# Expert weights in a four-slot ring in the order of use, and two narrow projections in column tiles

## The reference, cut to what matters

```python
h = rmsnorm(x, attn_norm)
parts = split(h @ w_in)              # 7448 columns: attention, GLA, DeltaNet, gates
merged = sum over three branches of sigmoid(gate_b) * (y_b @ w_br_b)
x = x + merged @ w_o
h = rmsnorm(x, ffn_norm)             # router: one of 4 groups, then 2 of its 8 experts
x = x + sum over the two experts e of weight * (silu(h @ w_gate_e[e]) * (h @ w_up_e[e])) @ w_down_e[e]
x = x + sigmoid(rmsnorm(x, ple_norm) @ w_ple_gate) * (p_i @ w_ple)
```

## Time and profile before

| | us |
|---|---|
| median of 3 runs | 1855.69 |
| lowest and highest | 1835.51, 2714.79 |
| profiled execution | 1843.19 |
| its span | 1841.5 |

### The profile page before, as it was taken

One profiled execution on the slowest core, in us unless ns is written; L12 is line 12 of the kernel. 1 busy time (PEld: TensorE's weight loads), 2 busy tenths in 40 slices (PEclk: granted clock), 3 DMA queues, 4 the chain that ended last, 5 costly groups with the idle time before them and its releaser, 6 DMA issues.

```text
span 1841.5 us, 19673 instructions
## 1 busy us (share of the span) xinstructions
PE 1456.5 (79%) x7340; PEld 720.6 (39%) x7341; DVE 395.5 (21%) x756; ACT 218.4 (12%) x417; POOL 38.0 (2%) x36
## 2 busy tenths in 40 slices
PE   7999999997655665566889999999976656665678
PEld 6657645452211221122476676454422212221223
DVE  3342514143000000000233425141420000000002
ACT  2121312110000000000211223111100000000001
POOL 0012000000000000000000110000000000000000
PEclk9999999998888888888989999999988888888889
DMA  7332033389999999999442320333899999999992
GB/s 249 114 137 92 1 137 137 115 353 365 402 410 409 410 410 410 409 410 407 156 145 92 137 92 6 142 127 137 349 364 410 410 409 410 410 410 409 410 398 87
DMA packets 153499, 501.19 MB, mean 272 GB/s; under 512 B 13763, under 2 KB 16229, under 8 KB 152293
## 3 DMA queue, kind: packets, MB, share of 16 engines
q1 hardware_dynamic: 153140, 498.72, 69.7%
q0 software_dynamic: 304, 1.76, 0.2%
HBM read 499.37 MB, written 1.05 MB: 272 GB/s over the span
## 4 chain that ended last, share of the span: by engine, by line
PE 50%; SPq 28%; DMA 14%; issue 4%; DVE 2%; ACT 1%; DVEq 0%; ACTq 0%
SPq L564 27%; PE ps L674 24%; DMA work<-in_w_gate_e 10%; PE ps L695 5%; PE ps L983 5%; PE ps L1120 3%; DMA ring<-in_w_down_e 2%; DMA work<-in_w_up_e 2%; SPq L508 1%; PE ps L816 1%; PE ps L1163 1%; PE ps L828 1%; ACT work L1210 1%; PE ps L1110 1%; PE ps L1104 1%
## 5 line engine op out<-in xcount | busy, mean ns | idle before, releaser
L1120 PE MATMUL ps<-work 128*32 128x512 f32 x2048 | 335.6, 793 | 277.9 <-DMA work<-in_w_up_e 159.3
L674 PE MATMUL ps<-ring,hT 128*128 128x512 f32 (+3 forms) x1152 | 452.3, 548 | 5.5 <-DVE hT L1510 5.5
L674 PEld LDWEIGHTS ps<-ring,hT 128*128 128x128 f32 x1152 | 208.4, 192 | 227.5 <-issue 223.4
L1210 ACT ACTIVATE work<-ps 128x512 f32<-128x512 f32 (+2 forms) x222 | 125.8, 589 | 1296.8 <-PE ps L1150 445.5
L1120 PEld LDWEIGHTS ps<-work 128*32 128x32 f32 x2048 | 65.5, 131 | 543.3 <-DMA work<-in_w_up_e 238.9
L1517 DVE SCALAR_TENSOR_TENSOR work<-work,ps 128x512 f32<-128x512 f32 (+1 forms) x52 | 37.9, 729 | 598.7 <-ACT work L1210 598.7
L1163 PE MATMUL ps<-ring,work 128*32 128x512 f32 x768 | 110.4, 719 | 39.9 <-DMA ring<-in_w_down_e 39.9
L695 PE MATMUL ps<-hT,ring 128*128 128x256 f32 x384 | 86.1, 387 | 1.8 <-DVE hT L1510 1.8
L983 PE MATMUL ps<-ring,work 128*128 128x512 f32 x192 | 84.7, 594 | 2.9 <-ACT work L1210 2.9
L695 PEld LDWEIGHTS ps<-hT,ring 128*128 128x128 f32 x384 | 74.3, 195 | 12.8 <-issue 1.3
L2000 DVE SCALAR_TENSOR_TENSOR work<-work,ps 128x512 f32<-128x512 f32 x16 | 11.0, 688 | 294.8 <-PE ps L1120 294.8
(11 more groups left out here) (262 smaller groups left out, 878.7 us busy)
## 6 DMA issues: line engine op xcount, KB each, us to landing
work<-in_w_gate_e SPq DMA_DIRECT2D x256, 512.0 KB, 15.0
work<-in_w_up_e SPq DMA_DIRECT2D x256, 512.0 KB, 14.6
ring<-in_w_down_e SPq DMA_DIRECT2D x192, 512.0 KB, 15.4
ring<-in_w_in SPq DMA_DIRECT2D x26, 2048.0 KB, 8.0
work<-in_w_down_e SPq DMA_DIRECT2D x64, 512.0 KB, 15.4
ring<-in_w_o SPq DMA_DIRECT2D x4, 2048.0 KB, 8.2
ring<-in_w_ple_gate SPq DMA_DIRECT2D x4, 2048.0 KB, 9.8
ring<-in_w_in SPq DMA_DIRECT2D x2, 2080.0 KB, 8.7
```

Source lines behind the costliest of these rows:

```text
L674: last = mm(ps[:, bank, at:at + n], hT[:, k, t * P:(t + 1) * P], w[:, k, c0:c0 + n], start=(k == 0), stop=(k == w.shape[1] - 1))
L1120: last = mm(ps[CAP * j:CAP * (j + 1), bank, :], xgT[:, 2 * c + k, CAP * j:CAP * (j + 1)], in_slot(c)[:, j, k, :], start=(c + k == 0), stop ...
L1210: return nc.scalar.activation(*args, **kw)
```

## The change

1. All expert weights go through one ring of four slots of 4 MB in the order of use: gate 0, gate 1, up 0, up 1, down 0, down 1. Chunk n lies in slot n mod 4 and is fetched when chunk n - 4 is used. A chunk is half of one matrix for four experts: four DMAs of 128 rows of 8 KB. The places are still 16 MB in all. Two rounds (12 chunks) make one turn of the loop.
2. Before the routing is known, gate and up of the first round are fetched (three chunks at `s_mT`, the fourth when `w_o` is used).
3. `w_ple` is fetched after chunk 11, behind a new signal that the routing buffers, which move into its slot, are free. Both halves of `w_ple_gate` are fetched when chunk 10 of the last pair is used.
4. Both narrow products are made in four column tiles: 32 columns of `w_in` stationary, 256 tokens streamed, tile q summing k-tiles 2q and 2q + 1. The four partial sums of `beta` are copied by ScalarE and added by a product with a table `stack8` after piece BVT; those of the low-rank part are added by the product with `wa2`, whose rows now stand four times, zero elsewhere. The bias is a product of its own.
5. `wa2` is loaded by four DMAs and the bias by a fifth, after a memset by GpSimd. `ye` lies in `hT`, its memset is gone.

```diff
+            def load_expert_chunk(n, experts):
+                half = n % 2
+                matrix = (w_gate, w_up, w_down)[n % 6 // 2]
+                place = expert_slot(n).rearrange("p (j n) -> p j n", j=TILES)
                 for j in range(TILES):
-                    src = one(matrix, experts[j])[:, :, c * 1024:(c + 1) * 1024].rearrange("l p n -> (l p) n")
+                    src = one(matrix, experts[j])[:, :, half * 2048:(half + 1) * 2048].rearrange("l p n -> (l p) n")
+                    sp.dma_start(place[:, j], src).then_inc(s_ex[n % 4].sem, 16)
...
             sp.wait_ge(s_mT.sem, s_mT.at(L, 4))
-            for c in range(4):
-                load_in(w_gate, first, c)
-            load_down(first, 0)
-            for c in range(3):
-                sp.wait_ge(s_static_used.sem, chunk_used(L, BEFORE_MOE + c - 3))
-                load_down(first, c + 1)
+            for n in (0, 1, 3):
+                load_expert_chunk(n, first[0])
+            sp.wait_ge(s_static_used.sem, chunk_used(L, J_WO1))
+            load_expert_chunk(2, first[0])
...
+            for n in range(4, CHUNKS):
+                sp.wait_ge(s_ex_used.sem, CHUNKS * base + (n - 3))
+                if n == CHUNKS - 1:
                     sp.wait_ge(s_units.sem, L + 1)
-                load_in(w_up, first, c)
-            with sp.Fori(0, n_rounds - 1) as g:
+                load_expert_chunk(n, first[n // 6])
+            sp.wait_ge(s_routed.sem, L + 1)
+            load_static(J_PLE)
+            with sp.Fori(0, n_pairs - 1) as g:
...
+                    sp.wait_ge(s_ex_used.sem, CHUNKS * prev + (n + CHUNKS - 3))
+                    load_expert_chunk(n, experts)
...
-            for j in (J_PG0, J_PLE, J_PG1):
-                sp.wait_ge(s_dn_used.sem, 4 * last + (j - J_PG0 + 2))
+            for j in (J_PG0, J_PG1):
+                sp.wait_ge(s_ex_used.sem, CHUNKS * last + CHUNKS - 1)
...
-            for t in range(T):
-                token_major(J_CG, t, 6, 0, 8, at=8 * t)
+            def small_columns(j, bank, c0):
+                w = slot_view(j)
+                for k in range(2):
+                    for q in range(4):
+                        last = mm(ps[32 * q:32 * (q + 1), bank, 0:SEQ], w[:, 2 * q + k, c0:c0 + 32],
+                                  hT[:, 2 * q + k, :], start=(k == 0), stop=(k == 1))
+                last.then_inc(s_small_p.sem, 1)
+            small_columns(J_CG, 6, 0)
...
-            for k in range(KT):
-                mm(ps[0:RANK, 7, 0:SEQ], w[:, k, 256:256 + RANK], hT[:, k, :], start=(k == 0), stop=(k == KT - 1))
+            small_columns(J_BVT, 7, 256 + RANK - 32)
...
+            pe.wait_ge(s_small.sem, L + 1)
+            pe.wait_ge(s_tab.sem, 16)
+            for t in range(T):
+                last = mm(ps[:, 6, SEQ + 8 * t:SEQ + 8 * (t + 1)], beta_parts[:, t * P:(t + 1) * P], table("stack8"),
+                          start=True, stop=True)
+            last.then_inc(s_beta_p.sem, 1)
...
-                        last = mm(ps[:, 0, t * 256:(t + 1) * 256], blrT[:, t * P:(t + 1) * P], wa2[:, :],
-                                  start=True, stop=True)
+                        mm(ps[:, 0, t * 256:(t + 1) * 256], lr_parts[:, t * P:(t + 1) * P], wa2[:, :],
+                           start=True, stop=False)
+                        last = mm(ps[:, 0, t * 256:(t + 1) * 256], table("ones")[0:1, :], ba_b[:, :],
+                                  start=False, stop=True)
...
+            act.wait_ge(s_beta_p.sem, L + 1)
+            fn(ba.rearrange("p t n -> p (t n)"), ps[:, 6, SEQ:SEQ + 16], ACT.Copy).then_inc(s_beta_e.sem, 1)
+            act.drain()
+            fn(beta, ba[:, :, 0:4], ACT.Tanh, scale=0.5).then_inc(s_beta_e.sem, 1)
```

More of the change, by code:

```diff
@@ L386, in _build @@
     s_slot = [signal(f"slot{i}_loaded") for i in range(3)]
-    s_in = [signal(f"expert_in_chunk{c}_loaded") for c in range(4)]
-    s_dn = [signal(f"expert_down_chunk{k}_loaded") for k in range(FT)]
+    s_ex = [signal(f"expert_slot{i}_loaded", 3) for i in range(4)]
     s_static_used = signal("static_chunk_used", NS)
@@ L545, in _ @@
                          ).then_inc(s_par.sem, 16)
-            sp.dma_start(wa2[:, :], one(a["wa2"], L).rearrange("l k n -> (l k) n")).then_inc(s_par.sem, 16)
+            src = one(a["wa2"], L).rearrange("l k n -> (l k) n")
+            sp.wait_ge(s_zero.sem, 1)
+            for j in range(4):
+                sp.dma_start(wa2[32 * j + 16:32 * (j + 1), :], src[0:RANK, :]).then_inc(s_par.sem, 16)
+            sp.dma_start(ba_b[:, :], src[RANK:RANK + 1, :]).then_inc(s_par.sem, 16)
             def load_static(j):
@@ L566, in in_place @@
-            def in_place(c):
-                return in_slot(c).rearrange("p j k n -> p j (k n)")
-            def load_in(matrix, experts, c):
-                load_quarters(matrix, experts, c, in_place(c), s_in[c])
-            def load_down(experts, k):
-                load_quarters(w_down, experts, k, down_slot(k), s_dn[k])
-            first = [L * E + j for j in range(TILES)]
-            sp.wait_ge(s_mT.sem, s_mT.at(L, 4))
-            for c in range(4):
-                load_in(w_gate, first, c)
@@ L580, in _ @@
-            load_down(first, 0)
-            for c in range(3):
-                sp.wait_ge(s_static_used.sem, chunk_used(L, BEFORE_MOE + c - 3))
-                load_down(first, c + 1)
+                    src = one(matrix, experts[j])[:, :, half * 2048:(half + 1) * 2048].rearrange("l p n -> (l p) n")
+                    sp.dma_start(place[:, j], src).then_inc(s_ex[n % 4].sem, 16)
+            first = [[L * E + TILES * r + j for j in range(TILES)] for r in range(2)]
+            sp.wait_ge(s_mT.sem, s_mT.at(L, 4))
@@ L605, in _ @@
-            last = plan(sp, L, LAST, FIRST_PASS - 1, 4096)
-            for j in (J_PG0, J_PLE, J_PG1):
-                sp.wait_ge(s_dn_used.sem, 4 * last + (j - J_PG0 + 2))
+                for n in range(CHUNKS):
+                    if n % 6 == 0:
+                        experts = [L * E + plan(sp, L, 8 * g + (8 + TILES * (n // 6) + j), 0, E - 1)
+                                   for j in range(TILES)]
+                    sp.wait_ge(s_ex_used.sem, CHUNKS * prev + (n + CHUNKS - 3))
+                    load_expert_chunk(n, experts)
@@ L1112, in scatter_tile @@
                 return last
-            def expert_in(bank, fill):
-                for c in range(4):
-                    pe.wait_ge(s_in[c].sem, 64 * fill)
-                    for k in range(2):
-                        for j in range(TILES):
-                            last = mm(ps[CAP * j:CAP * (j + 1), bank, :], xgT[:, 2 * c + k, CAP * j:CAP * (j + 1)],
-                                      in_slot(c)[:, j, k, :], start=(c + k == 0), stop=(c == 3 and k == 1))
-                    last.then_inc(s_in_used.sem, 1)
@@ L1124, in _, with expert_in @@
-            pe.wait_ge(s_sel0.sem, L + 1)
-            gather().then_inc(s_ga0.sem, 1)
-            pe.wait_ge(s_tbl.sem, L + 1)
-            base = plan(pe, L, BEFORE, 0, 4096)
-            last_round = plan(pe, L, LAST, FIRST_PASS - 1, 4096)
-            n_rounds = plan(pe, L, ROUNDS_AT, FIRST_PASS, ROUNDS_LIMIT)
-            with pe.Fori(0, n_rounds) as g:
-                gg = base + g
-                pe.wait_ge(s_xg.sem, gg + L + 1)
-                pe.wait_ge(s_swT.sem, gg + 1)
-                expert_in(6, 2 * gg + 1)
-                pe.wait_ge(s_hg.sem, gg + 1)
-                expert_in(7, 2 * gg + 2)
-                pe.wait_ge(s_ye.sem, gg + 1)
+            def expert_in(pp, r, up):
+                bank = 6 + up
+                for c in range(2):
+                    n = 6 * r + 2 * up + c
+                    pe.wait_ge(s_ex[n % 4].sem, 192 * pp + 64 * (n // 4 + 1))
+                    for k in range(4):
+                        for j in range(TILES):
+                            last = mm(ps[CAP * j:CAP * (j + 1), bank, :], xgT[:, 4 * c + k, CAP * j:CAP * (j + 1)],
+                                      in_slot(n)[:, j, k, :], start=(c + k == 0), stop=(c == 1 and k == 3))
+                    last.then_inc(s_ex_used.sem, 1)
```

251 lines of the change are left out of this document (137 added, 114 removed).

## The result

The changed kernel took 1816.66 us (median of 4 runs, 1815.70 to 1817.57) where the kernel before took 1848.36 us (median of 4 runs, 1835.51 to 2714.79). The ratio is 0.9836, with a 95% interval of 0.9803 to 0.9870: 1.6% less, and the whole interval lies within 2%. The ratio compares executions in the fast state alone, so the one of 2714.79 us is not in it. The forecast was 1808.6 us in a range of 1788 to 1837. The profiled execution took 1817.57 us (span 1815.9), against 1843.2 (1841.5): 25.6 us less where the sum said 34.6. So the case that I forecast is the one that came, and 9 us of it did not.

What follows compares the result with a forecast made beforehand. TensorE was taken to bound the static part, the DMA engines' rate the expert part. From 1843.2 us, 25.6 (experts) and 10.4 (narrow columns) off and 1.4 (start) on gave 1808.6 us, range 1788 to 1837.

Steps and rivals of the forecast that it cites:

- the case that I forecast: Whole kernel: faster rate, narrow columns paying, 1808.6 us; between 1800 and 1818 by itself, chance 0.58.
- The rate: Expert stream: 8 KB rows raise 409.6 GB/s to 422, a round from 61.44 to 59.6 us; 13.3 us per layer.
- Rival 1: Expert stream: the rate gains nothing or little; 1835 us unchanged, 1825 with 3.5 ns per packet; chance 0.16.
- The middle and both dips: Expert stream: no gap after prefetch, second DMA dip gone, slots free in time with 18 us of slack.
- The start of the stream: Start of the expert part: the stream starts 5.3 us after the first gate product, t0.
- The last landing: End of the expert stream: last chunk there at t0 + 445.6, with 0.5 us to land.
- The last product: Last down product of a layer: taken as 6.0 us, between 3.6 at full and 6.8 at lower clock.
- `w_ple` early: Expert stream: fetching `w_ple` early gains nothing at the end and costs 2.5 us of saturated stream.
- The narrow columns: Static part: column tiles save 4.3 and 2.6 us, additions cost some; net 5.2 us per layer, 10.4 in both.
- Rival 2: Static part: narrow columns do not pay, as tiles do not overlap or the decay chain catches TensorE; 1819 us, chance 0.12.
- The start: Kernel start: four more DMAs and a wait before the first `w_in` load make TensorE 1.4 us later, bounds 0 and 2.1.
- rival 3: Expert part: TensorE at the lower clock bounds it, a round takes 64 us; 1879 us in all, chance 0.06.

Runs made afterwards that it cites:

- run 5: The changed kernel with `w_ple` fetched after the last expert chunk, between the halves of `w_ple_gate`: 1818.44 us, ratio 0.9849 to the kernel before.
- runs 7 and 11: 7: changed kernel plus filler products before two TensorE waits and late `w_ple`, 1810.93 us; 11: that with `wa2` loads moved and more fillers, 1811.14 us.
- run 4: The changed kernel with the narrow columns as in the kernel before: 1822.34 us, ratio 0.9868 to the kernel before.

## Why the prediction was right, and where it was off

**The rate, right.** I took 422 GB/s and 59.6 us a round from a line through two row sizes (the 2 and 4 KB rows fix it; the 16 KB readings, 421 and 431, only span it). Measured 421 and 59.73. With 4 KB rows it is 409 again, with 16 KB rows 428. Per packet and engine, 8192 x 16 / 421.3 = 311.1 ns, so the cost that does not grow with the bytes is 2 x 160.0 - 311.1 = 8.9 ns, and from 8 to 16 KB 2 x 311.1 - 16384 x 16 / 428 = 9.7 ns, against the 9.4 of the forecast. The Trainium skill (DMA: Bandwidth & Descriptors, Why small descriptors are slow) names about 3 cycles per packet, by its 850 MHz an estimate of 3.5 ns; the runs show 8.9 to 9.7 ns, and the measurement decides. Rival 1 is out. What the cost is inside the DMA engines no run shows.

**The middle and both dips, right.** The ring never ran dry and no slot came free too late.

**The start of the stream, right.** Forecast for t0 + 5.3. Chunk 4 was issued at 414.40 and the rate was full from 417 on, with 184 GB/s in the 2 us before: as if it had started at t0 + 5.4.

**The last landing, the mis-sized term.** It came at t0 + 448.7, not 445.6. With the start above, 185.6 MB at 421 GB/s are through at t0 + 446.3; I had 445.1 for this, and the step from 422 to 421 makes 1.0 of the 1.2 us. The other 1.9 us lie between this and the product, for which I had given 0.5 and which took 2.4: the rate is full until 856.0, t0 + 445.3, and the product still starts only at 859.41. In these last 3.4 us the DMA share is 0.63 and the rate 209 GB/s. The packets in the trace say why: 24 to 27 of 8 KB end in each half us until 857.0, then 17, 11, 9 and 4, each about as long as before, and the last ends at 858.86. So from 857 on part of the engines had nothing left of chunk 11 while others still had, and the next load comes late. From the last packet to the product it is 0.55 us, so the 0.5 was right for that; what I had not counted is that the engines do not end together. In the kernel before the rate stayed at 391 to 418 up to the last down product, since the next load was queued by then, so this tail could not be seen there.

**The last product, mis-sized both ways.** I took 6.0 us. It took 3.64 at full clock in layer 0 and 5.24 in layer 1, which is more than the difference between the two layers' -12.1 and -10.9. In layer 0 this paid for the late landing. The two products, layer 0 and layer 1:

```profile
859.41 3.64 PE L1183 MATMUL ps<-work 128*32 128x512 f32 x32 [2.16 <-DMA work<-in_w_down_e]
...
1762.34 5.24 PE L1183 MATMUL ps<-work 128*32 128x512 f32 x32 [2.54 <-DMA work<-in_w_down_e]
```

**`w_ple` early, right.** 2.5 us of stream in the sum, 2.4 in run 5.

**The narrow columns, the size right up to `wa2` and wrong in the total.** Up to the product with `wa2` the lead was 6.2 us, as the terms say (4.3 + 2.6 - 0.8 = 6.1). But the 4.3 was read wrongly: of the 5.3 us that I gave the old narrow instructions of piece CG, they took 3.6, and 1.7 were the fall of the clock behind them (0.57 over 62 to 66). The new columns are rid of that fall too, which I had not foreseen. The tiles overlap, no gap stands where the tiling changes (59.29 + 1.07, next at 60.29), and the longer chain to the decays never held TensorE. The Trainium skill (TensorEngine Tiling (Array Packing), Key Properties) would have had a drain there; the rows have none. The bias cost 1.35 us and not 0.9. What failed is the silent step "TensorE has no gap here, so time saved there counts": between CG and t0 the same instructions do not always take the same time. A fall to 1.2 GHz at 195 took 3.25 us and one before t0 1.6 more. Ahead of these falls the columns are worth 4.8 us in layer 0, so 9.6 for both and not 10.4, and 1.7 of each 4.8 is the fall at 62 that is gone. What they are worth in the total the runs give only as 5 to 12 us, by whether the clock falls and where. Rival 2, which had the columns pay nothing for other reasons, gave 1819 and so came near the time by the wrong mechanism.

**The start, wrong.** I charged 1.4 us for four more DMAs and a wait ahead of `w_in`. The first load was issued at 6.28 instead of 4.37, and landed at 15.25 instead of 15.11. The DMA engines were already busy with `x` and `rows` at that time (a DMA share of 1.05 and 379 GB/s at 4 to 6 us), so an issue 1.9 us earlier had nothing to gain. The 1.3 us charged too much made up part of what the sum was short of, by luck.

**TensorE as the bound (rival 3), out.** 38 of 60 us busy in a round, with the clock at 0.84 of full speed (0.83 over the whole stream).

What stays open is what decides where the clock falls. Fillers removed the fall at 195 in all five profiles with new columns, where four of six without them had it; in three of the five the clock was then low at 390 to 398, in the other two at 402 to 406. These two (runs 7 and 11) are the ones that had started slowly, and run 5, slow at the start and without fillers, has its fall at 402 too. I did not separate this further. What makes the clock fall is not shown: the same idle time passed with and without a fall, and the fall at 62 with the old columns has no idle time ahead of it.

## What to carry to other kernels

Where a stream of loads bounds a stage, measure the rate at two row sizes, put a line through packet time against bytes, and read the gain of the next size off it; it held here to 1 GB/s up to 16 KB, but larger rows also mean coarser chunks, and the first and the last of them stand on the path. Count a saving on a nearly gapless TensorE with the granted clock of the whole way to the next real wait, since a fall of the clock behind a short gap can take it back; a filler product in that gap held the clock there in five of five profiles, but it must end before the wait does, and the clock can fall further on. Look at single executions before a difference of medians is set against a sum: two groups 6 us apart can hide in one median. Instructions moved ahead of a load cost nothing while the DMA engines are already full.

## What the runs showed of the hardware that I had not expected

- The end of a saturated stream is ragged: 3.4 us at a mean of 209 GB/s before the last chunk of 4 MB was usable, after 439 us at 421, with fewer and fewer packets ending (25, 17, 11, 9, 4 in half us).
- After the same 2.02 us of idle TensorE the granted clock over 195 to 203 was 0.57 to 0.68 in four of six profiles with the new columns and no filler, and 1.00 in the other two and in the two with the old columns. In layer 1 it fell there in one of these two as well (run 4, 0.57 over 1107 to 1115). With fillers in the gap it was 1.00 in all six.
- At the start TensorE ran at half speed for 4 to 5 us longer in four of fourteen profiles (10 instructions in the place of 20, 16 to 20 us). The records of the granted clock begin with its first rise, at 19.7 to 20.4 us there and at 14.1 to 16.1 elsewhere, and the clock's column reads 1.00 ahead of it.
- Behind 32 matmul instructions of 8 columns, 0.11 us apart, the clock fell to 1.2 GHz with no idle time of TensorE ahead of it, in both layers of all three profiles that had them.
